# The first layer's two attentions: projections and half the output product laid between attention steps

## What is computed

```
aq, ak, av, bq, bk, bv = split_cols(h @ w_in, AB_SPLITS)      # six projections of 512 columns
# a: 4 heads with two maps each (rotary), values 128 wide
ao = softmax(q0 k0) v - lam * softmax(q1 k1) v                # causal
ao = rms(ao, g_sub) * (1.0 - lam_init)
# b: 8 heads of 64 (rotary), causal, weighted by how many of three dilated windows hold the key
bo = dilated_attention(rope(bq), rope(bk), bv)
y  = concatenate([ao, bo]) @ w_out                            # (256, 1024) @ (1024, 1024)
h  = h + rms(y, g_mix_post)                                   # then the MLP of this layer
```

## Time and profile before

| | us |
|---|---|
| median of 3 runs | 2370.42 |
| lowest, highest | 2366.43, 2375.66 |
| the profiled execution, whole | 2366.39 |
| its span (first to last instruction) | 2364.5 |
| span of the part that the change touches (rows of the section below) | 113.1 |

### The profile page before, as it was taken

How to read it: one execution, slowest core, us unless ns; L and a number is a source line. 1 busy time by engine, 2 the same in 40 slices (tenths; PEclk the granted TensorE clock), 3 DMA queues, 4 the chain that set the end, 5 groups by cost and what they waited for, 6 DMA issues and landing times.

```text
span 2364.5 us, 27466 instructions
## 1 busy us (share of the span) xinstructions
PE 1915.7 (81%) x11188; PEld 1213.3 (51%) x11188; DVE 840.3 (36%) x1513; ACT 699.7 (30%) x1235; POOL 191.7 (8%) x191
## 2 busy tenths in 40 slices
PE   6998999999986556656665666557989999989999
PEld 4765978789941111111111111116749985658985
DVE  4354677875540000000000000006546643546643
ACT  4344267675320000000000000004345432355531
POOL 1200022252020000000000000001000000010000
PEclk9999899999998888788878787888989999999999
DMA  8542243345579999999999999994505544314552
GB/s 348 220 145 112 95 124 117 112 141 189 213 310 428 427 428 429 427 429 429 428 429 427 429 429 428 430 429 160 189 18 184 182 178 181 143 37 161 187 193 110
DMA packets 66004, 619.05 MB, mean 262 GB/s; under 512 B 8032, under 2 KB 16736, under 8 KB 21360
## 3 DMA queue, kind: packets, MB, share of 16 engines
q1 hardware_dynamic: 54304, 598.98, 62.7%
q10 hardware_dynamic: 9248, 10.49, 1.8%
q0 software_dynamic: 2352, 8.19, 1.0%
HBM read 616.52 MB, written 1.11 MB: 261 GB/s over the span
## 4 chain that ended last, share of the span: by engine, by line
PE 55%; DMA 37%; DVE 4%; ACT 3%; issue 1%; SPq 0%; ACTq 0%; DVEq 0%
DMA ring<-in_w_edown 18%; DMA ring<-in_w_eup 17%; PE bank L496 12%; PE bank L497 11%; PE bank L498 11%; PE bank L584 2%; PE bank L2706 2%; PE bank L2449 2%; PE bank L2472 2%; PE bank L555 2%; PE bank L1189 1%; PE bank L1704 1%; DMA ring<-in_w_ada 1%; PE bank L569 1%; PE bank L1097 1%
## 5 line engine op out<-in xcount | busy, mean ns | idle before, releaser
L467 DVE TENSOR_TENSOR ring_parts<-ring,ring_parts 128x2048 fp32r<-128x2048 f32 x108 | 245.1, 2274 | 158.6 <-ACT ring_parts L461 154.1
L461 ACT CAST ring_parts<-ring 128x2048 fp32r<-128x2048 f32 (+1 forms) x136 | 251.0, 1848 | 158.8 <-DMA ring<-in_w_mlp_out 88.8
L2518 DVE TENSOR_TENSOR work<-bank,work 128x512 f32<-128x512 f32 x14 | 9.7, 691 | 802.7 <-PE bank L2449 802.7
L2449 PE MATMUL bank<-ring,work 128*32 128x512 f32 x1024 | 167.4, 787 | 141.6 <-DMA ring<-in_w_egate 78.1
L2472 PE MATMUL bank<-ring,work 128*32 128x512 f32 x1024 | 170.8, 802 | 107.0 <-DMA ring<-in_w_edown 100.9
L478 POOL TENSOR_TENSOR ring_parts<-ring,ring_parts 128x512 fp32r<-128x512 f32 x96 | 126.6, 1352 | 1274.9 <-ACT ring_parts L461 1274.9
L2449 PE MATMUL bank<-work 128*32 128x512 f32 x1024 | 146.7, 702 | 78.1 <-DMA work<-in_w_eup 65.7
L496 PE MATMUL bank<-hT_hi,ring_parts 128*128 128x256 f32 (+1 forms) x576 | 193.2, 335 | 0.0
L496 PE MATMUL bank<-hn_hi,ring_parts 128*128 128x256 f32 x640 | 184.3, 288 | 3.8 <-DVE hn_lo L685 3.8
L498 PE MATMUL bank<-hT_hi,ring_parts 128*128 128x256 f32 (+1 forms) x576 | 184.3, 320 | 0.0
L497 PE MATMUL bank<-hT_lo,ring_parts 128*128 128x256 f32 (+1 forms) x576 | 184.2, 320 | 0.0
(11 more groups left out here) (384 smaller groups left out, 3172.8 us busy)
## 6 DMA issues: line engine op xcount, KB each, us to landing
ring<-in_w_edown SPq DMA_DIRECT2D x64, 2048.0 KB, 26.4
work<-in_w_egate SPq DMA_DIRECT2D x32, 2048.0 KB, 26.0
ring<-in_w_egate SPq DMA_DIRECT2D x32, 2048.0 KB, 25.8
ring<-in_w_eup SPq DMA_DIRECT2D x32, 2048.0 KB, 26.3
work<-in_w_eup SPq DMA_DIRECT2D x32, 2048.0 KB, 26.1
ring<-in_w_mlp_in SPq DMA_DIRECT2D x32, 1024.0 KB, 4.8
ring<-in_w_mlp_out SPq DMA_DIRECT2D x32, 1024.0 KB, 4.8
ring<-in_w_ada SPq DMA_DIRECT2D x12, 2048.0 KB, 9.1
```

What stands on the lines that cost most here:

```text
L461: act.copy(halves_of(name, ring_parts)[1], halves_of(name, ring)[0]).then_inc(hi_made, 1)
L467: dve.tensor_tensor(lo, halves_of(name, ring)[0], hi, ALU.subtract).then_inc(lo_made, 1)
L2449: last = pe.matmul(bank[which][32 * n:32 * n + 32, :], xg[:, e2, 2 * c + k2, :], w[:, k2, 512 * n:512 * n + 512], start=c == 0 and k2 == 0 ...
```

## The change

In A, the query and key projections of b (8 feature groups, their copies, swaps and rotations, and four splits of weight chunks) move into the hooks of A's steps. In B, the value projection of b (2 token groups, in 4 pieces) stands in steps 1 to 4 of PE, and the first half of the output product (contraction blocks 0 to 3, 4 pieces) in steps 10, 12, 14 and 16. The second half follows B. The banks are dealt out anew: A has scores in 0 and 1, transposes in 2 and 3, values in 4 alone, projections in 5 and 6, swaps in 7 alone; B has scores in 0 and 1, transposes in 2 alone, values in 3 alone; the transposes of A's result use bank 7 in place of 5.

```diff
-        AA = Attention(8, 2, ..., (3, 6))
+        AA = Attention(8, 2, ...,
+                       (2, 3), (0, 1))
...
-                       ..., (3, 6))
-        AB.hooks = head_values(AB, v_ab["b"], PT_b, 8, True, counted["values"], lambda blk: obT[:, 4 + blk, :])
+                       ..., (2,), (0, 1))
+        AB.hooks = head_values(AB, v_ab["b"], PT_b, 8, True, counted["values"], lambda blk: obT[:, 4 + blk, :], (3,))
...
+        def b_ahead_pe(pe, step):
+
+            pieces = {1: ("bq", 0), 2: ("bq", 1), 4: ("bq", 2), 5: ("bq", 3), 7: ("bk", 0), 8: ("bk", 1), 10: ("bk", 2), 12: ("bk", 3)}
+            swaps = {3: 0, 5: 1, 7: 2, 9: 3, 11: 4, 13: 5, 15: 6, 17: 7}
...
+                pe.wait_ge(gemm_freed, n - 1)
...
+        def b_ahead_act(act, step):
+            ropes = {2: 0, 3: 1, 5: 2, 7: 3, 9: 4, 11: 5, 13: 6, 15: 7}
+            splits = {4: "bk_0", 6: "bk_1", 10: "bv_0", 14: "bv_1"}
...
+        def b_ahead_dve(dve, step):
+            ropes = {4: 0, 6: 1, 8: 2, 10: 3, 12: 4, 14: 5, 16: 6, 18: 7}
+            splits = {5: "bk_0", 7: "bk_1", 11: "bv_0", 15: "bv_1"}
...
-                if u >= 2:
-                    pe.wait_ge(av_stored, u - 1)
+                if u >= 1:
+                    pe.wait_ge(av_stored, u)
...
-            pe.wait_ge(gemm_freed, GROUP["bv"] + TT)
-            pe.wait_ge(rope_done, rope_n["dve"])
-            att_pe(pe, AA, scores_a, value_a)
+            pe.wait_ge(gemm_freed, GROUP["av"] + TT)
+            pe.wait_ge(rope_done, 24)
+            att_pe(pe, AA, scores_a, value_a, each_step_of(AA, b_ahead_pe))
...
+                if half and (t, h) == (1, 1):
+                    turn_tile(pe, ATTENTION, 0)
+                for k in range(4 * half, 4 * half + 4):
+                    last = pe.matmul(bank[4 + 2 * t + h][:, :], obT[:, k, t * P:(t + 1) * P], w[:, k, :], start=k == 0, stop=k == KT - 1)
...
+            def b_along_pe(pe, step):
+                values = {1: (0, 0), 2: (0, 1), 3: (1, 0), 4: (1, 1)}
+                outs = {10: (0, 0), 12: (0, 1), 14: (1, 0), 16: (1, 1)}
...
             pe.wait_ge(av_stored, 8)
+            pe.wait_ge(rope_done, 32)
...
-            rows_product(pe, "o0", obT, lambda pe: turn_tile(pe, ATTENTION, 0))
+            out_half(pe, 1)
...
-            att_act(act, AB, AB.hooks[2])
+            att_act(act, AB, AB.hooks[2], {6: lambda act: take_ab_values(act, "b")})
...
-            att_dve(dve, AB, AB.hooks[1], between={3: scale_a, 8: lambda dve: take_a(dve, 0), 11: lambda dve: take_a(dve, 1)})
+            att_dve(dve, AB, AB.hooks[1], between={2: scale_a, 6: lambda dve: take_a(dve, 0), 8: lambda dve: take_a(dve, 1)})
```

More of the change, by code:

```diff
@@ L2792, in ab_proj_act @@
             act.wait_ge(lam_sub_sum, 2)
             act.activation(lam[:, 2:4], lam[:, 0:2], ACT.Exp).then_inc(lam_sub_root, 1)
+        def b_ahead_pe(pe, step):
+            pieces = {1: ("bq", 0), 2: ("bq", 1), 4: ("bq", 2), 5: ("bq", 3), 7: ("bk", 0), 8: ("bk", 1), 10: ("bk", 2), 12: ("bk", 3)}
+            swaps = {3: 0, 5: 1, 7: 2, 9: 3, 11: 4, 13: 5, 15: 6, 17: 7}
+            if step in swaps:
+                rope_pe(pe, GROUP["bq"] + swaps[step], "swap32")
+            if step in pieces:
+                name, b = pieces[step]
+                n = GROUP[name] + b
+                w = split_chunk(pe, f"{name}_{b // 2}")
+                pe.wait_ge(gemm_freed, n - 1)
+                for k in range(KT):
+                    last = product3(pe, gemm_bank(n)[:, 0:L], [x[:, k, b % 2 * P:b % 2 * P + P] for x in w], [x[:, k, :] for x in AB_ROWS],
+                                    k == 0, k == KT - 1)
+                last.then_inc(gemm_ready, 1)
@@ new lines, in b_ahead_act @@
+        def b_ahead_act(act, step):
+            ropes = {2: 0, 3: 1, 5: 2, 7: 3, 9: 4, 11: 5, 13: 6, 15: 7}
+            splits = {4: "bk_0", 6: "bk_1", 10: "bv_0", 14: "bv_1"}
+            if step in ropes:
+                rope_act(act, GROUP["bq"] + ropes[step])
+            if step in splits:
+                split_upper(act, splits[step])
+        def b_ahead_dve(dve, step):
+            ropes = {4: 0, 6: 1, 8: 2, 10: 3, 12: 4, 14: 5, 16: 6, 18: 7}
+            splits = {5: "bk_0", 7: "bk_1", 11: "bv_0", 15: "bv_1"}
+            if step in ropes and ropes[step] < 4:
+                rope_dve(dve, tb("ab_qc"), tb("ab_qs"), [(q_ab["b"][:, ropes[step], :], 0, 128)])
+            elif step in ropes:
+                rope_dve(dve, tb("ab_kc"), tb("ab_ks"), [(k_ab["b"][:, ropes[step] - 4, :], 0, 128)])
+            if step in splits:
+                split_lower(dve, splits[step])
@@ new lines, in b_values_pe @@
+        def b_values_pe(pe, u, i):
+            n = GROUP["bv"] + i
+            w = split_chunk(pe, f"bv_{u}")
+            if u == 0:
+                pe.wait_ge(gemm_freed, n - 1)
+            for k in range(4):
+                last = product3(pe, gemm_bank(n)[:, :], [x[:, 4 * u + k, i * P:(i + 1) * P] for x in AB_ROWS], [x[:, k, :] for x in w],
+                                u == 0 and k == 0, u == 1 and k == 3)
+            if u == 1:
+                last.then_inc(gemm_ready, 1)
+            elif i == TT - 1:
+                last.then_inc(chunk_used, 1)
@@ L2795, in ab_proj_dve, with each_step_of @@
+        def each_step_of(A, of_step):
+            return {step: lambda eng, step=step: of_step(eng, step) for step in range(A.units * A.parts + TURN + 2)}
         def ab_proj_dve(dve):
```

103 lines of the change are left out of this document (60 added, 43 removed).

## The result

The changed kernel takes 2377.9 us (median of 9 runs, 2375.8 to 2380.2) against 2370.7 of the kernel before in the same job: a ratio of 1.0032, 95% interval 1.0021 to 1.0042. It is 7 us slower. Forecast was a gain of 3.7, and 2377.9 lies outside the range (2355 to 2376).

What follows compares the result with a forecast made beforehand. PE bounds the products; in A and B it waits for short round trips. Parts and clock, -3.0 - 2.8 + 2.1 = -3.7, take the profiled 2366.4 to 2362.7; the median, 4.0 higher, is 2366.7 us, range 2355 to 2376.

Steps and rivals of the forecast that it cites:

- Part 1: A with b's queries and keys: ends at T = 47 us from the stage's start, giving back 3 us.
- DVE busy over 80% from the fourth turn on: Sign of being right: in A of the changed kernel DVE is busy over 80% from its fourth turn.
- A over 51 us: Sign of being wrong: A with b's keys takes over 51 us, where 46 to 48 was expected.
- Part 2: B with b's values and half the output: ends at T = 89.6; with the second half, gives back 2.8 us.
- steps 10 to 16 are PE's: In B: four output pieces of 3.47 us plus 1.5 to 1.8 of PE's own work each, 20 us.
- Part 3: Second half of the output behind B: 17.8 us, with 3.0 of the wait for the norm bare.
- The clock: PE's clock falls to half in A's tail, before the value pieces: costs 2.1 us, bounds 0 to 13.
- 0.50 beyond the value pieces: Sign of being wrong: PE's clock is at 0.50 beyond b's value pieces in B.
- the clock or a transfer did it: Reading set beforehand for a time above 2376 us: the clock or a transfer is the reason.
- The clock stays at half: Rival: clock at half from A's tail into the output pieces, costing 8.3 to 13 us, total 2373 to 2378; chance 0.1.
- Round trips too short: Rival: 0.35 us more on each of A's and B's 16 turns, +5.6 us, giving 2372; chance 0.2.
- No overlap: Rival: moved pieces do not overlap at all; stage as before plus 3.0 us, giving 2373; chance 0.03.

Runs made afterwards that it cites:

- e1: Changed kernel with DVE's copy of each value in A moved to the start of its turn; 2366.9 us, ratio to the kernel before 0.9978 to 1.0006.
- e10: Changed kernel with A's values alternating between two banks and transposes using one; 2368.3 us, ratio to the kernel before 0.9987 to 1.0015.
- e2: Kernel before with only the four output pieces put in B, with the banks they need; 2375.3 us, ratio 1.0020 to 1.0054.
- e3: Changed kernel without output pieces in B, the output product whole behind it; 2376.8 us, ratio to the kernel before 1.0019 to 1.0054.
- e4: As e1, with the lower parts of A's four splits made by GpSimd; 2372.9 us, ratio to the kernel before 1.0002 to 1.0029.
- e9: As e1, with matmuls that nothing reads in A's tail and ahead of the transposes behind B; 2368.9 us.
- e11: Changed kernel with copy first, a split behind A, three output pieces behind scores, the fourth behind B, unread matmuls in A's tail; 2358.5 us.

## Why the prediction failed

- **Part 1, the step that failed.** It predicted A to end at T = 47; measured 57.3. Of the stage's miss of 14.6 (124.1 against 109.5), 10.3 are here. The walk let DVE's masks, PE's scores and the swaps wait for each other, and counted the single value bank only for "the last two values". Five waits of 12.0 us in all hang on it (1.4, 3.7, 1.4, 4.8 and 0.6), with a fall of the clock in each of the two long ones, since the copy ends DVE's turn and the next value stands ahead of the next scores. With that wait gone the same walk is off by 0.7 to 1.3 (47.7 and 48.3), and 6.1 of waits for DVE stand at the swaps where it put them. The sign "DVE busy over 80% from the fourth turn on" was false for the same reason: from that turn's first mask to the end of A it is 62%, in e1 and e10 78 and 80%. The sign of being wrong, A over 51 us, came.
- **Part 2.** 42.6 was forecast for B, measured 47.2, and 44.4 in e10, where the clock holds. So 1.8 is the walk (the two waits of 1.13 were not in it) and 2.8 the clock, most of it in the first two value pieces. The part "steps 10 to 16 are PE's" was nearly right (2.3 us idle in 20.7), and hid the question that mattered: whether the pieces fill anything. They don't (e2, e3). Of B's 5.6 idle, 2.3 lie between the pieces, 1.1 in steps 5 to 9 and 2.0 in the tail, the last two where no piece stands.
- **Part 3.** 17.8 forecast, 18.1 in e10, the wait of 3.0 is 3.04. Missing was its second price: behind that wait the level fell in three of the seven traces that have it (e1, e2, e4), and the last piece takes 5.3 us in e2 in place of 3.6.
- **The clock.** 2.1 was too small. Against e10, PE's same work took 8.0 longer: 3.7 in A, 2.8 in B, 1.5 behind; e10 is not free of it either (0.93 in A). The 3.7 stand against e1 as well (3.1), the rest does not. The fall in A's tail was foreseen with its place; the one in A's middle came with the value bank's wait, and that at B's end was not foreseen, though "0.50 beyond the value pieces" was named as a sign of being wrong.
- **The sum.** With 47, 42.6, 17.8 and 2.1 the stage would have been 109.5. It is 110.2 in e10 and 124.1 in the changed kernel. That e10 comes so near is luck in part: the walk without a clock term gives 107.4, and the 2.1 stand there for what the three parts were short (0.7, 1.8 and 0.3). With A's 57.3 in the sum the forecast would have been 2377.0; a walk that held the bank as well would have found the 5.9 of waits in this, not the clock. The last sentence of the prediction, that above 2376 "the clock or a transfer did it", names half: it was a bank, and the clock behind it.
- **The rivals.** "The clock stays at half" came in part (12.8 us at 0.50 from A's tail on), as a consequence; its 2373 to 2378 holds the measured 2377.9, but by another sum. "Round trips too short" was worth 1.8 in B and 0.7 to 1.3 in A of the 5.6, by e10 and e1. "No overlap" had a chance of 0.03 and was right for the output pieces; in A, too, no idle time was filled (5.6 before, 8.5 in e10), and what A wins with the wait gone is PE's busy time.
- **Left open.** The same list from B on has a spell at 0.50 at the end of B in e1 and none in e10, and none of the twelve runs tells why. e1's runs spread over 15 us (2360.5 to 2375.6); its traced execution, 2374.6, is one of the longest and has three such spells in the stage.

## What to carry over

Where a change takes banks away, list for each bank the instruction that frees it and where that stands in its engine's turn: a copy at the end of a turn of 4 us costs nothing with two banks and everything with one, and moving it to the front of the turn costs nothing. Work that is to hide a round trip belongs behind the instruction that starts the trip, not ahead of it (here 1.3 us of B, and too little for the medians by itself). And split the length of a stage into PE's busy time and its idle time in both kernels: where the work is the same, a rise in busy time is the clock. In A it added 3.1 to 3.7 us to 5.9 us of waits. Look at more than one execution before you price it for a whole stage.

## What the runs showed of the hardware

- GpSimd and DVE (e4): with GpSimd on tensor operations of 1.26 to 1.46 us between SBUF tiles, DVE's instructions from SBUF to SBUF of 128x128 and more take 1.25 to 1.49 us in place of 0.28 to 0.48, all eleven that met one in the four places. Masks and a copy, which read PSUM, take 0.28 to 0.42 as always; a reciprocal of 128x2 stays at 0.16, and a product of 128x1 takes 0.16 to 0.85. The Trainium skill says, on the page "SBUF — State Buffer", section "SBUF: two separate sides", that for an operation of DVE with two SBUF inputs or in a two-port mode the port pair shared with GpSimd is locked for a whole instruction and the loser is blocked; the trace agrees for these eleven. For L1123, which has one tensor input, no run shows in which mode it runs.
- The clock and banks: in e10, B cycles through one transpose bank and one value bank with waits of 0.4 to 1.1 us, idle 5.6 of 44.4, and the level stays at 1.00 throughout. By the rule that the prediction cited from the Trainium skill (page "TensorE: Matmul & The Clock Gate", section "A second HAM failure mode: psum-queue depth-cycling") it should have gone back and forth. Other traces agree with the rule: at the end of nearly the same B the level fell behind waits of 0.45 to 1.13 us alone in the changed kernel, e1, e4 and e9. In A and at the norm it fell in or right behind longer waits: 3.7 and 4.8 us for the bank (changed kernel), 4.3 for the rotation (e1), 3.0 for the norm (e2). No run tells what decides it.
- In A's tail, 24 matmuls of 128x256 in 3.1 us put off a fall by some 5 us, counted from the start of A, and did not prevent it (e9 against e1); 33, spread over five gaps, with 2.3 us less to wait, went with no fall at all (e11). One execution of each was traced.
